# One change in an fp32 three-block forward pass: output projections begun block by block, two reorderings, and a shorter launch

## The reference, cut to what matters

```
for l in range(2):                                   # first block
    h = rms_norm(x); z = h @ w_in                    # 7436 columns
    four mixers of 256 columns each: sparse attention with a relative-position
        bias, retention, rwkv7, short convolution
    merged = sum_m sigmoid(gate_m) * (mixer_m @ w_branch_m)
    x += rms_norm(merged @ w_mix_out)
    x += rms_norm(cross_attention(rms_norm(x), rms_norm(mem)))   # 4 heads, @ wo
    x += rms_norm(relu(rms_norm(x) @ w1)**2 @ w2)
# second block: forgetting attention, a gated linear recurrence, a 31-tap
# convolution; their concatenation @ w_out; then a mixture of 32 experts
a = exp(log_a); beta = sqrt(1 - a*a)                 # in the recurrence
```

## Time and profile before

| | |
|---|---|
| median of three runs | 2109.21 us |
| the profiled execution | 2104.69 us, its span 2102.9 us |
| TensorE (PE) busy | 1915.1 us (91%) |
| VectorE (DVE) busy | 1426.7 us (68%) |
| ScalarE (ACT) busy | 1168.5 us (56%) |
| chain that ended last | PE 65%, DVE 22%, ACT 8%, issue 2% |
| mean granted TensorE clock | 0.961 |

### The profile page before, as it was taken

One profiled execution on the slowest core, in us unless ns is written; L12 is line 12 of the kernel. 1 busy time (PEld: TensorE's weight loads), 2 busy tenths in 40 slices (PEclk: granted clock), 3 DMA queues, 4 the chain that ended last, 5 costly groups with the idle time before them and its releaser, 6 DMA issues.

```text
span 2102.9 us, 30304 instructions
## 1 busy us (share of the span) xinstructions
PE 1915.1 (91%) x12946; PEld 1747.3 (83%) x12946; DVE 1426.7 (68%) x1425; ACT 1168.5 (56%) x1310; POOL 76.5 (4%) x94
## 2 busy tenths in 40 slices
PE   4999997988999889997997999897779999999997
PEld 3989997987998889997997999796668888888885
DVE  3686547545555677637645555755679999999995
ACT  2644344544444554333644444454368888888884
POOL 0000013000000000013000000000000000000000
PEclk9999998998999999999998999998879999999998
DMA  7333374524554333356542555332259999999993
GB/s 265 127 141 136 119 266 162 200 101 142 193 189 159 156 141 131 127 178 243 186 159 105 190 195 181 134 121 86 94 224 374 375 375 380 377 379 374 375 391 135
DMA packets 64524, 440.87 MB, mean 210 GB/s; under 512 B 7372, under 2 KB 7372, under 8 KB 14592
## 3 DMA queue, kind: packets, MB, share of 16 engines
q1 hardware_dynamic: 55296, 399.63, 50.6%
q0 software_dynamic: 8096, 35.30, 4.5%
q10 hardware_dynamic: 992, 3.93, 0.5%
HBM read 428.61 MB, written 10.23 MB: 209 GB/s over the span
## 4 chain that ended last, share of the span: by engine, by line
PE 65%; DVE 22%; ACT 8%; issue 2%; POOL 1%; DMA 1%; DVEq 0%; ACTq 0%; POOLq 0%
PE psum L188 64%; DVE ring_low L202 6%; ACT hl L198 3%; DVE arena L212 3%; DVE ht L202 2%; DVE rounded L202 2%; DVE rounded L212 2%; DVE arena L202 2%; ACT arena L198 1%; PE psum L192 1%; POOL arena L202 1%; DVE hl L202 1%; ACT rounded L198 1%; DVE arena L225 1%; DVE resid L202 1%
## 5 line engine op out<-in xcount | busy, mean ns | idle before, releaser
L202 DVE TENSOR_TENSOR hl<-ring,hl 128x2048 fp32r<-128x2048 f32 (+1 forms) x190 | 433.9, 2286 | 350.7 <-ACT hl L198 350.3
L188 PE MATMUL psum<-ht,hl 128*128 128x256 f32 x4992 | 630.2, 288 | 15.4 <-DVE hl L202 9.7
L188 PEld LDWEIGHTS psum<-ht,hl 128*128 128x128 f32 x4992 | 616.2, 195 | 25.1 <-DVE hl L202 10.3
L198 ACT ACTIVATE hl<-ring 128x2048 fp32r<-128x2048 f32 (+1 forms) x286 | 536.3, 1896 | 150.7 <-PE psum L188 122.9
L188 PE MATMUL psum<-hl,ax 128*128 128x512 f32 (+1 forms) x1608 | 351.9, 355 | 6.4 <-DVE ax L202 5.0
L198 ACT ACTIVATE arena<-psum 128x512 f32<-128x512 f32 (+5 forms) x232 | 121.0, 522 | 418.5 <-PE psum L188 405.5
L188 PEld LDWEIGHTS psum<-hl,ax 128*128 128x128 f32 x1608 | 264.8, 192 | 47.3 <-DVE ax L202 5.3
L202 DVE TENSOR_TENSOR ring_low<-ring,hl 128x2048 fp32r<-128x2048 f32 x96 | 215.3, 2285 | 19.3 <-ACT hl L198 19.1
L188 PE MATMUL psum<-arena 128*128 128x128 f32 (+6 forms) x1520 | 190.8, 291 | 30.1 <-ACT arena L198 23.5
L188 PEld LDWEIGHTS psum<-arena 128*128 128x128 f32 (+2 forms) x1520 | 174.7, 179 | 41.6 <-ACT arena L198 25.2
L188 PE MATMUL psum<-hl,ht 128*128 128x256 f32 (+1 forms) x1056 | 132.2, 287 | 26.8 <-DVE ht L212 24.0
(11 more groups left out here) (121 smaller groups left out, 1897.7 us busy)
## 6 DMA issues: line engine op xcount, KB each, us to landing
ring<-W SPq DMA_DIRECT2D x284, 1024.0 KB, 5.1
arena<-W SPq DMA_DIRECT2D x48, 1024.0 KB, 7.5
ht_raw<-W SPq DMA_DIRECT2D x46, 1024.0 KB, 7.8
gate_d<-arena POOLq DMA_DIRECT2D x32, 256.0 KB, 3.8
arena<-gate_d POOLq DMA_DIRECT2D x8, 1024.0 KB, 8.0
gn<-GB POOLq DMA_DIRECT2D x10, 512.0 KB, 4.1
arena<-GB POOLq DMA_DIRECT2D x6, 512.0 KB, 4.9
ring<-W SPq DMA_DIRECT2D x4, 512.0 KB, 4.5
```

The lines of the kernel that those rows point to most:

```text
L188: return Nothing() if self.e is None else self.e.matmul(o, a, b, start=start, stop=stop, skip_group_check=skip_group_check)
L198: return self.e.activation(o, a, f, bias=bias, scale=scale)
L202: return Nothing() if self.e is None else self.e.tensor_tensor(o, a, b, op)
```

## The change

It has five parts. (1) `tok_out` takes `ready`: for the first unit TensorE waits for one block of the input at a time and multiplies it for both token halves before the next; `mixout` and `xout` use it, `bout` doesn't. (2) The fourth `vx` unit moves behind the transposes of the shares on TensorE and ScalarE, and VectorE scales the shares after one unit instead of four. (3) At launch X is loaded first, each engine waits only for what it needs, one unit is split ahead of the norm's cut and two right behind it, and `kcks` is multiplied before the `bias` products. (4) In the second block the four `unit()` calls move behind the gelu on ScalarE and behind `log_weight(3)` on VectorE. (5) 1 - a*a is formed as (a*a + 1) * tanh, without the reciprocal; the sign goes into the root's scale.

```diff
@@ tok_out @@
                 for q in range(2):
-                    u, *_ = unit()
-                    for t in range(2):
-                        part(u, q, t)
+                    u, wh, wl = unit()
+                    if ready and q == 0:
+                        for kk in range(4):
+                            pe.wait_ge(s_dve, V[ready[0], kk, ready[1]])
+                            for t in range(2):
+                                ts = slice(128 * t, 128 * t + 128)
+                                ins = mm3(psum[:, banks[(*name, t, 0)], 0:256],
+                                          [((lhs[0][:, k, ts], lhs[1][:, k, ts]), (wh[:, k, :], wl[:, k, :]))
+                                           for k in (2 * kk, 2 * kk + 1)], kk == 0, kk == 3)
+                                if kk == 3:
+                                    ins.then_inc(s_pe, P(*name, t, 0))
+                    else:
+                        for t in range(2):
+                            part(u, q, t)
@@ TensorE @@
             pe.wait_ge(s_const, 16)
-            pe.wait_ge(s_par, 16)
-            pe.wait_ge(s_x, 16)
-            pe.wait_ge(s_once, 16)
-            b = bank("rowb")
...
+                if l == 0:
+                    pe.wait_ge(s_par, 16)
+                    pe.wait_ge(s_once, 16)
+                    b = bank("rowb")
+                    mm(psum[0:4, b, :], [(R("rel")[0:32, :], m0.onehot[0:32, :])]).then_inc(s_pe, P("rowb"))
                 norm(L.nmix.xn, "mix", l)
                 if l == 0:
+                    pe.wait_ge(s_dve, V["mix", l])
+                    proj(hTv, "kcks", l)
                     pe.wait_ge(s_hank, 32)
...
-                pe.wait_ge(s_dve, V["merged", l])
-                tok_out(hTv, "mixout", l, between=lambda: norm(L.mem, "mem", l))
+                tok_out(hTv, "mixout", l, between=lambda: norm(L.mem, "mem", l), ready=("merged", l))
...
-                for g in range(4):
+                for g in range(3):
                     proj_rows(axv, "vx", g, l)
...
+                proj_rows(axv, "vx", 3, l)
                 for h in range(4):
                     b = bank("ox", h, l)
                     pe.wait_ge(s_act, A["pxT", 1, 3, l])
+                    pe.wait_ge(s_act, A["vx", h, l])
...
-                pe.wait_ge(s_dve, V["ox", 3, l])
-                tok_out(hTv, "xout", l)
+                tok_out(hTv, "xout", l, ready=("ox", l))
@@ ScalarE @@
+            ac.dma_start(Xv, x_in.rearrange("b (t p) d -> p (b t) d", t=2)).then_inc(s_x, 16)
             ac.dma_start(cst[:, :], CS).then_inc(s_const, 16)
             ac.dma_start(par[:, :], PR).then_inc(s_par, 16)
-            ac.dma_start(Xv, x_in.rearrange("b (t p) d -> p (b t) d", t=2)).then_inc(s_x, 16)
             ac.dma_start(arena[:, 0:896], CO[:, 0:896]).then_inc(s_once, 16)
-            ac.wait_ge(s_const, 16)
-            ac.wait_ge(s_par, 16)
             ac.wait_ge(s_x, 16)
-            ac.wait_ge(s_once, 16)
-            ac.wait_ge(s_pe, P["rowb"])
-            copy(m0.rowb[0:4, :], psum[0:4, banks["rowb",], :], "rowb")
-            gone("rowb")
...
                         norm(Xv, L.nmix, t, "mix", l)
+                    upper()
+                    ac.wait_ge(s_const, 16)
+                    ac.wait_ge(s_par, 16)
+                    ac.wait_ge(s_once, 16)
+                    ac.wait_ge(s_pe, P["rowb"])
+                    copy(m0.rowb[0:4, :], psum[0:4, banks["rowb",], :], "rowb")
+                    gone("rowb")
                     for t in range(2):
                         norm_cut(hTv, t, "mix", l)
-                if l == 0:
+                    for _ in range(LOOK):
+                        upper()
                     ac.wait_ge(s_bias, 16)
...
-                for g in range(4):
+                def values(g):
                     unit()
...
+                for g in range(3):
+                    values(g)
...
+                values(3)
...
             copy(b2.xg, half(banks["xg",]), "xg")
             gone("xg")
-            for _ in range(4):
-                unit()
...
-            act(t1, t1, ACT.Sqrt, "ustd")
+            act(t1, t1, ACT.Sqrt, "ustd", scale=-1.0)
             ac.wait_ge(s_dve, V["gelu"])
             act(t3, t3, ACT.Tanh, "gelu", scale=math.sqrt(2.0 / math.pi))
+            for _ in range(4):
+                unit()
             weights(3)
@@ VectorE @@
-            ve.wait_ge(s_const, 16)
-            ve.wait_ge(s_par, 16)
             ve.wait_ge(s_x, 16)
-            ve.wait_ge(s_once, 16)
...
                         norm(Xv, L.nmix, t, "mix", l)
+                    lower_part()
+                    ve.wait_ge(s_const, 16)
+                    ve.wait_ge(s_par, 16)
+                    ve.wait_ge(s_once, 16)
                     for t in range(2):
                         norm_cut(hTv, t, "mix", l)
+                    for _ in range(LOOK):
+                        lower_part()
...
-                for g in range(4):
-                    unit()
+                unit()
                 ve.wait_ge(s_act, A["sxexp", l])
                 rec(L.f[:, :, 3:4], L.f[:, :, 2:3])
                 tt(L.pr, L.pr, wide(L.f[:, :, 3:4], 256), MUL, "px", l)
+                for g in range(1, 4):
+                    unit()
...
             log_keep(2)
             unit()
-            for _ in range(4):
-                unit()
             ve.wait_ge(s_act, A["lam"])
...
-            ts(t1, t3, -1.0, None, ADD, None)
-            rec(t1, t1)
-            stt(t1, t3, 2.0, t1, MUL, MUL, "uvar")
+            tt(t1, aL, aL, MUL)
+            stt(t1, t1, 1.0, t3, ADD, MUL, "uvar")
...
             log_weight(3)
+            for _ in range(4):
+                unit()
             ve.wait_ge(s_act, A["ya", 2])
```

More of the change, by code:

```diff
@@ L631, in norm, with tok_out @@
                         ins.then_inc(s_pe, P(*name, t, j))
-            def tok_out(lhs, *name, between=None):
+            def tok_out(lhs, *name, between=None, ready=None):
                 for t in range(2):
@@ L675, in tensor @@
             pe.wait_ge(s_const, 16)
-            pe.wait_ge(s_par, 16)
-            pe.wait_ge(s_x, 16)
-            pe.wait_ge(s_once, 16)
-            b = bank("rowb")
-            mm(psum[0:4, b, :], [(R("rel")[0:32, :], m0.onehot[0:32, :])]).then_inc(s_pe, P("rowb"))
             for l in range(2):
                 L = layers[l]
+                if l == 0:
[3 more added lines that the diff above has]
+                    mm(psum[0:4, b, :], [(R("rel")[0:32, :], m0.onehot[0:32, :])]).then_inc(s_pe, P("rowb"))
                 norm(L.nmix.xn, "mix", l)
                 if l == 0:
+                    pe.wait_ge(s_dve, V["mix", l])
+                    proj(hTv, "kcks", l)
                     pe.wait_ge(s_hank, 32)
@@ L690, in tensor @@
                 fill = filler(l)
-                pe.wait_ge(s_dve, V["mix", l])
-                proj(hTv, "kcks", l)
+                if l:
+                    pe.wait_ge(s_dve, V["mix", l])
+                    proj(hTv, "kcks", l)
                 proj(hTv, "q", l)
@@ L1580, in keys @@
                     gone("kx", g, l)
-                ac.wait_ge(s_dve, V["merged", l])
+                ac.wait_ge(s_dve, V["merged", 3, l])
                 norm(Xv, L.nxa, 1, "xa", l, after=("mixout", l))
@@ L2300, in low @@
                     ve.wait_ge(s_act, A["merged", jj, l])
-                    stt(hTv[1][:, js, :], first[:, js, :], 0.5, hTv[0][:, js, :].bitcast(F32), MUL, SUB, "merged", l, after=False)
+                    stt(hTv[1][:, js, :], first[:, js, :], 0.5, hTv[0][:, js, :].bitcast(F32), MUL, SUB, "merged", jj, l, after=False)
                 for jj in range(4):
@@ L2712, in gates_back @@
                 gp.dma_start(flat(layers[l].Gt[:, 8 * m:8 * m + 8, :]), gate_d[:, 2048 * m:2048 * m + 2048]).then_inc(s_gin[m], 16)
-            gp.wait_ge(s_const, 16)
-            gp.wait_ge(s_par, 16)
-            gp.wait_ge(s_x, 16)
-            gp.wait_ge(s_once, 16)
             gain("mix0")
```

## The result

The changed kernel takes 2059.03 us (median of 4 runs, 2055.42 to 2062.17) against 2108.58 us (2103.8 to 2111.39, 4 runs) for the kernel before: ratio 0.9767, 95% interval 0.9741 to 0.9792, 49.6 us less. The forecast was 2060. The profiled execution took 2062.17 us with a span of 2060.3, 42.6 less than the span of before.

What follows compares the result with a forecast made beforehand. Chains across engines, not busy shares, were taken as the bound. Launch 12.5, mixout 10.2, xout 10.4 and second block 13.7 sum to 46.8: 2057.9 from the profile, 2062.4 from the median, so forecast 2060, range 2052 to 2076 us.

Steps and rivals of the forecast that it cites:

- Launch, 12.5: At launch, loading X first and reordering splits and products starts vg at 43.2 instead of 55.98, winning 12.5 us.
- my upper bound of 14: Launch: the most it could win, 14 us, with X at 8.6 and a clock that holds.
- the bias products: Launch: the four bias products behind kcks take 4.63 us and end at 34.4.
- mixout, 5.1 a layer: Before mixout: starting by blocks ends the first unit at 342.5, not 347.6, winning 5.1 us a layer.
- My third rival: TensorE's clock stays at 1.2 GHz through the projection's four units after block-wise starts: 23 us slower, about 2132; chance 0.04.
- xout, 5.2 a layer: Before xout: the moved fourth vx unit and earlier shares start xout at 456.8, not 462.02, winning 5.2 us a layer.
- my upper bound of 5.5: Before xout: the idles of 1.72, 2.37 and 1.41 us are all that can go, together 5.5.
- Second block, 13.7: Second block: moving the four split calls removes ScalarE's wait for a weight load and TensorE's idle, winning 13.7 us.
- ScalarE holds most of that: Second block: the form without reciprocal saves 3.1 us, mostly held by ScalarE's exponential, logarithm and table loads.
- Rival (2): Block-wise starts win nothing, as the wait passes to hidden work; gives back 20.6 us, about 2081; chance 0.06.
- rival (1): Launch or second block: one rearranged stage wins half, 6 to 7 us less, about 2067; chance 0.17.
- rival (4): The pieces cancel against something later, as experts bound by another start: within 0.5% of before; chance 0.03.

Runs made afterwards that it cites:

- f2: Changed kernel with the weight loads from the fifth unit on held back until bias_d is written; 2063.3 us, ratio 0.9787.
- u2: Changed kernel with the block-wise starts of mixout and xout alone undone, in both layers; 2070.18 us, ratio 0.9832.
- f4: Changed kernel with seven products of constants on TensorE in the pause before mixout, in both layers; 2056.11 us, ratio 0.9751.
- u3: Changed kernel with the order of the last vx unit and the shares alone undone, block-wise start kept; 2071.27 us, ratio 0.9833.
- u4: Changed kernel with the second block's four split calls alone put back, the reciprocal still away; 2071.54 us, ratio 0.9833.
- u5: Changed kernel with the reciprocal form of the input's scale put back, everything else as changed; 2060.51 us, ratio 0.9771.
- a0: The changed kernel run again, unaltered, as the mark for the kernels beside it; 2059.32 us, ratio 0.9773.
- u1: Changed kernel with the launch alone put back in its old order; 2072.95 us, ratio 0.9836.
- f3: Changed kernel with vg's weight unit split before the wait for bias_d, and bout begun by blocks too; 2051.51 us, ratio 0.9736.
- f5: f3 with products of constants in TensorE's pauses before kcks, before each mixout and in the second block; 2045.37 us, ratio 0.9701.

## Why the prediction was right

The result, 2059.03, lies 1 us from the forecast of 2060. That is closer than the parts were: by the experiments and stages the launch and `xout` won more than I had, `mixout` and the second block less, and the errors cancelled. That is luck. The mechanisms, one by one:

**Launch, 12.5.** Right by mechanism, somewhat small by size: undone alone it costs 13.6. Up to the row of 64 products, nine profiles with the new launch or a variant of it (all but the first and f2) stand at 83.4 to 84.3, where the two old launches have 98.90 and 99.04. That is 14.6 to 15.6 earlier, beyond my upper bound of 14. The term that I had too large is the bias products: I took the 4.63 us of the earlier trace rows, and in every profile of the new launch but one they took 2.74 (u2: 2.85). Why they were slower in the kernel before is open: the granted clock is 1.00 in both. What runs behind them, `q` and `kw`, ends by so much sooner.
The first profile shows only 8.2. There `vg` started 2.0 us earlier than I had it, but I costed its products at the earlier trace rows's full clock, and did not ask what a pause before it would do to the clock. That one row and the 80 products behind it lost 6.5 us.

**mixout, 5.1 a layer.** The start came 4.96 us earlier, as worked out. TensorE does not catch up with VectorE, as I had it. The term that was too small is the unit itself: I left it at the 7.6 us of before, and it takes 8.0 and 8.1 in the first profile's two layers, 8.0 to 8.6 in all profiles with the block-wise start and no fill before it. The stage is worth 4.1 to 4.5 by the changed kernel's two profiles against before, and 3.2 to 4.2 by u2. My third rival fell: in both layers of every profile the second unit's 48 products run at full clock (5.7 us), so the low one never outlasts the first.

The Trainium skill ("TensorE: Matmul & The Clock Gate", section "A second HAM failure mode: psum-queue depth-cycling") says that short idles between groups of products make the clock swing. The runs here do not show it. In the changed kernel no idle stands between the groups, so the rule is hardly put to the test. In f4 the groups of 12 have idles of 0.62 and 0.30 us between them, and the granted clock is 1.00; but that is three groups, once in each layer.

**xout, 5.2 a layer.** It is 6.3 (37.96 to 31.67), above my upper bound of 5.5. I added the row lengths as they stand, but each row's last product has a modelled tail that overlaps what follows: 17.61 + 1.91 + 6.00 + 7.07 is 32.59, and `xout` starts after 31.68. That is 0.9 of the 1.1 us that I was off. The two halves aren't equal: u2 gives the early start 1.8, u3 gives the order 6.2 by itself, since its pauses brought the low clock too and lost the 1.7 that the early start wins. Their sum, 8.0, is more than the 6.3 of both.

**Second block, 13.7.** 12.5 and 13.2 to `bout` in the two profiles of the changed kernel (11.0 to 13.3 in the others with this second block), 12.2 by u4. The moved units carry it, through ScalarE's wait for the load. From `taps(1)` to the variance's product it takes 42.76 us before, 42.95 in u4 without the reciprocal, 30.81 in u5 with the units moved and the reciprocal back, and 29.59 in the changed kernel. So the reciprocal is worth 1.2 once the units are moved, as my "ScalarE holds most of that" had it, and nothing that shows by itself. The splits did not push the centring out: it comes 13.2 us earlier relative to `taps(1)`, the logits 13.4.

**Sum.** 46.8 predicted. The four pieces undone one by one cost 13.6 + 10.9 + 12.0 + 12.2 = 48.7 us, all of them together 48.5 (2107.77 less 2059.32). That they agree so well is partly chance: u2 and u3 count 1.7 us of each `xout` twice, 3.4 in all, and each of the four differences is good to 2 us. But nothing large is given back. By the spans of the two profiles the whole is 42.6 and 44.2; a0's six stages win 47.6, and 3.1 goes between the layers, most of it in the row of 64 (7.34 us for 4.74). Rival (2), no gain from the blocks, falls with u2; rival (1), half a stage, with u1 and u4; rival (4), a cancelling later on, with the result and the unchanged experts.

What stays open is what decides on which pause the clock falls. Before `kcks`, in ten profiles with this launch, the 48 products took 6.0 us three times, behind pauses of 1.74 to 1.91 us, and 7.4 to 7.6 us seven times, behind pauses of 1.76 to 2.21 us. Length alone doesn't tell. In two of the seven, f3 and f4, the granted clock stands at 1.00 all the while (f3: 9 products from 22 to 24 us, where the first profile has 16), so there the slow clock is read from the products' time alone, and another cause isn't ruled out.

## What to carry to other kernels

Where an engine waits for the last of several equal blocks, start by blocks in the order in which they are made; it is worth the wait for the others, less what the slow clock takes. Fill TensorE's pauses with later work or even products of constants, but expect a gain only where TensorE, not VectorE, is the next bound. Cost a moved product at both levels of the clock when a new pause stands before it, and judge single stages by several profiles.

## What the runs showed of the hardware

A pause of about 2 us on TensorE can be enough for the lower clock level: 48 identical products behind it took 6.02 us in one profile of the changed kernel and 7.50, with 0.50 granted from 24 to 26 us, in the other. The Trainium skill ("TensorE: Matmul & The Clock Gate", section "Part 1: The HAM clock gate (the "warmup" mystery)") says that how many products run slow at first differs from run to run of one kernel; these two profiles agree. How long it can last is larger than I expected: about 0.50 from 41.2 to beyond 54 us, with TensorE busy throughout, cost `vg` 5.0 us and the 80 products behind it 1.5 (8.20 for 6.66).

The same 768 KB write took 3.5 to 4.3 us in seven profiles of the new launch and 4.9 to 7.2 in the four where it was issued 1.1 to 1.6 us earlier, beside the weight loads. So what a faster `kcks` wins is lost in waiting for the write: `vg` starts between 40.5 and 41.3 in all of these profiles but f5, which splits that unit before the wait and loses the time at the next load.
